# Four attention heads of a query block in a row: one finish for the four, the least score as bias, one dummy product

## What is computed

```python
def masked_softmax(s, mask):
    s = jnp.where(mask, s, NEG_INF)
    e = jnp.where(mask, jnp.exp(s - jnp.max(s, -1, keepdims=True)), 0.0)
    return e / jnp.maximum(jnp.sum(e, -1, keepdims=True), 1e-30)
...
# MLA, a block of 128 queries: q and k 96 wide
p = masked_softmax(s.astype(jnp.float32) * scale, k_pos[None, :] <= q_pos[:, None])
return jnp.einsum('bhqk,bkhd->bqhd', p.astype(v.dtype), v)
...
# NSA: compressed keys (31), selected blocks, window; a gate each
o = g[:, :, 0] * o_cmp + g[:, :, 1] * o_slc + g[:, :, 2] * o_win
...
# DSA: an index score picks the 128 best keys of each query
rel = jax.nn.relu(jnp.einsum('bqhd,bsd->bqhs', qi, k_idx).astype(jnp.float32))
score = jnp.einsum('bqh,bqhs->bqs', wi, rel)
score = jnp.where(k_pos[None, None, :] <= q_pos[None, :, None], score, NEG_INF)
_, idx = lax.top_k(score, n_top)
```

## Time and profile before

| | |
|---|---|
| time, median of 3 runs | 3823.72 us (3822.14 to 3828.15) |
| the profiled execution | 3826.97 us, span 3825.2 us |
| TensorE matmuls | 3499.9 us busy, 91% of the span |
| TensorE weight loads | 2786.0 us, 73% |
| VectorE | 1767.2 us, 46% |
| ScalarE | 1441.1 us, 38% |
| GpSimd | 181.0 us, 5% |
| mean granted clock of TensorE | 0.95 of the full one |

### The profile page before, as it was taken

How to read it: one execution, slowest core, us unless ns; L and a number is a source line. 1 busy time by engine, 2 the same in 40 slices (tenths; PEclk the granted TensorE clock), 3 DMA queues, 4 the chain that set the end, 5 groups by cost and what they waited for, 6 DMA issues and landing times. The chain is left out here.

```text
span 3825.2 us, 44194 instructions
## 1 busy us (share of the span) xinstructions
PE 3499.9 (91%) x16088; PEld 2786.0 (73%) x16126; DVE 1767.2 (46%) x2931; ACT 1441.1 (38%) x2357; POOL 181.0 (5%) x127
## 2 busy tenths in 40 slices
PE   7999889988999899989898899969999897889998
PEld 5888666766888688867576688847777675677886
DVE  4333447735333433342883533346665446444333
ACT  3332325454332333232446433235555335423321
POOL 0001011002001000100200200100000000000000
PEclk9999998989999999999898999989999998899999
DMA  3232210002232233222000222211121222222231
GB/s 132 96 103 90 94 61 1 1 19 76 99 103 95 67 99 103 95 91 74 1 1 12 72 97 99 99 43 62 62 68 62 71 74 69 76 73 94 99 103 68
DMA packets 75812, 277.38 MB, mean 73 GB/s; under 512 B 12432, under 2 KB 13968, under 8 KB 74896
## 3 DMA queue, kind: packets, MB, share of 16 engines
q1 hardware_dynamic: 75664, 275.45, 21.7%
HBM read 273.32 MB, written 2.10 MB: 72 GB/s over the span
## 5 line engine op out<-in xcount | busy, mean ns | idle before, releaser
L318 DVE TENSOR_TENSOR wlo<-raw,whi 128x1024 fp32r<-128x1024 f32 (+2 forms) x464 | 609.9, 1314 | 1019.6 <-ACT whi L314 1019.5
L346 PE MATMUL ps<-xh,whi 128*128 128x512 f32 x2384 | 941.7, 395 | 50.8 <-DVE wlo L318 38.2
L347 PE MATMUL ps<-xl,whi 128*128 128x512 f32 x2384 | 934.0, 392 | 0.0
L348 PE MATMUL ps<-xh,wlo 128*128 128x512 f32 x2384 | 933.7, 392 | 0.0
L314 ACT ACTIVATE whi<-raw 128x1024 fp32r<-128x1024 f32 (+2 forms) x464 | 515.3, 1111 | 621.5 <-PE ps L348 613.5
L346 PEld LDWEIGHTS ps<-xh,whi 128*128 128x128 f32 x2384 | 451.8, 190 | 154.1 <-DVE wlo L318 30.2
L347 PEld LDWEIGHTS ps<-xl,whi 128*128 128x128 f32 x2384 | 451.8, 190 | 95.9 <-issue 2.9
L348 PEld LDWEIGHTS ps<-xh,wlo 128*128 128x128 f32 x2384 | 451.2, 189 | 94.9
L346 PE MATMUL ps<-ffn_hh,whi 128*128 128x512 f32 x880 | 345.4, 393 | 11.1 <-DVE ffn_hl L719 11.1
L347 PE MATMUL ps<-ffn_hl,whi 128*128 128x512 f32 x880 | 343.1, 390 | 0.0
L348 PE MATMUL ps<-ffn_hh,wlo 128*128 128x512 f32 x880 | 343.1, 390 | 0.0
(11 more groups left out here) (361 smaller groups left out, 4535.5 us busy)
## 6 DMA issues: line engine op xcount, KB each, us to landing
raw<-in_ffn_up SPq DMA_DIRECT2D x216, 512.0 KB, 3.4
raw<-in_ffn_down SPq DMA_DIRECT2D x80, 704.0 KB, 4.0
raw<-in_ssm_in SPq DMA_DIRECT2D x44, 512.0 KB, 3.4
raw<-in_mix_in SPq DMA_DIRECT2D x40, 512.0 KB, 3.4
raw<-in_lru_in SPq DMA_DIRECT2D x20, 512.0 KB, 3.3
raw<-in_mix_out SPq DMA_DIRECT2D x16, 512.0 KB, 3.6
raw<-in_ssm_out SPq DMA_DIRECT2D x16, 512.0 KB, 3.3
raw<-in_lru_out SPq DMA_DIRECT2D x8, 640.0 KB, 3.9
```

What stands on the lines that cost most here:

```text
L318: dve.tensor_tensor(self.core.wlo[:, u % HALF, 0:width], self.core.raw[:, u, 0:width], self.core.whi[:, u % HALF, 0:width].bitcast(F32), A ...
L346: pe.matmul(out, c.whi[:, h, w], xh[:, k0 + k], start=first and k == 0, stop=False)
L347: pe.matmul(out, c.whi[:, h, w], xl[:, k0 + k], start=False, stop=False)
L348: mm = pe.matmul(out, c.wlo[:, h, w], xh[:, k0 + k], start=False, stop=last and k == nk - 1)
```

## The change

- The units stand in groups of four: the four heads of one query block in one branch. MLA's four blocks come first, then for each block of NSA its compressed, selected and window group, then DSA's four blocks.
- The scale is taken into the queries with a minus sign (where they are split or evacuated), and the masks are added with the opposite sign through a negative identity. So the scores are negative, the least of a row takes the place of the greatest, and it is the bias of the exponential (scale -1) as it stands: `bias` is gone. The compressed units get a 32nd column with a bound for rows without any key.
- The four heads of a group write their values into one bank, 256 columns, and their sums into one tile of four columns. `finish` runs once for a group: clamp (compressed groups), reciprocal, gate, one product of 256 columns with the factors repeated over 64 columns each, and, for selected and window groups, a separate addition. It stands between `largest` and `take` of the unit 4n + 5, with n the group.
- `keep_clock` issues one dummy product a unit instead of two.
- Two further phases (stick breaking, L1383, and the state-space groups, L1801) use the negative identity with their masks' signs turned; the set-up makes the bf16 constants with two activations instead of one.

```diff
-                act.activation(c.kb_all[:], c.consts[:, 0:N_BF16 * P], ACT.Copy).then_inc(ph["kb_done"], 1)
+                act.activation(c.kb["nident"], c.k["ident"], ACT.Copy, scale=-1.0).then_inc(ph["kb_done"], 1)
+                act.activation(c.kb_all[:, P:], c.consts[:, P:N_BF16 * P], ACT.Copy).then_inc(ph["kb_done"], 1)
...
+    def group(mixer, b, q, k, mask, at, width, v, gate=None, first=True, least=None):
+        units = [dict(q=q(h), k=k(h), mask=mask, at=at, width=width, least=least or width, v=v(h), h=h) for h in range(HEADS)]
+        groups.append(dict(units=units, mixer=mixer, b=b, gate=gate, first=first, clamp=least is not None))
+    for b in range(QB):
+        own, past = slice(b * P, (b + 1) * P), slice(0, (b + 1) * P)
+        group(0, b, lambda h: [m.qm[:, h, own]], lambda h: [m.km[:, h, past]], c.kb["negd"], b * P, (b + 1) * P,
+              lambda h: [m.vm[:, j, h * HD:(h + 1) * HD] for j in range(b + 1)])
+    for b in range(QB):
+        own, past = slice(b * P, (b + 1) * P), slice(0, (b + 1) * P)
+        q = lambda h: part(NSAQ + h // 2, h, own)
+        group(1, b, q, lambda h: part("kc", h, slice(0, NCMP + 1)), c.kb["cmpm"][:, b * (NCMP + 1):(b + 1) * (NCMP + 1)], 0, NCMP,
+              lambda h: [m.vc[:]], gate=m.tok[:, b, GATE:GATE + HEADS], least=NCMP + 1)
+        for br, (kt, vt) in enumerate(((KSLC, VSLC), (KWIN, VWIN))):
+            g = GATE + (br + 1) * HEADS
+            group(1, b, q, lambda h: part(kt, h, past), c.kb["negd"], b * P, (b + 1) * P,
+                  lambda h: [m.tok[:, j, vt:vt + HD] for j in range(b + 1)], gate=m.tok[:, b, g:g + HEADS], first=False)
+    for b in range(QB):
+        own, past = slice(b * P, (b + 1) * P), slice(0, (b + 1) * P)
+        group(2, b, lambda h: part(DSAQ + h // 2, h, own), lambda h: [x[64 * (h % 2):64 * (h % 2) + 64, past] for x in m.split[DSAK][:2]],
+              c.kb["negd"] if b == 0 else allowed[b], 0, (b + 1) * P, lambda h: [m.tok[:, j, DSAV:DSAV + HD] for j in range(b + 1)])
+    return groups
...
-                    keep_clock(c, pe, 6 + u % 2, 2)
+                    keep_clock(c, pe, 6 + u % 2, 1)
...
-                    if u >= 2:
-
-                        pe.wait_ge(ph["y_done"], u - 1)
+                    if u % HEADS == 0 and u >= 2 * HEADS:
+                        pe.wait_ge(ph["y_done"], u // HEADS - 1)
                     w = min(P, x["width"])
+                    h = x["h"]
                     for j, v in enumerate(x["v"]):
-                        mm = pe.matmul(c.ps[:, 4 + u % 2, 0:HD], pt[0:w, u % 2, j * P:(j + 1) * P], v, start=j == 0, stop=j == len(x["v"]) - 1)
+                        mm = pe.matmul(c.ps[:, 4 + u // HEADS % 2, h * HD:(h + 1) * HD], pt[0:w, u % 2, j * P:(j + 1) * P], v, start=j == 0, stop=j == len(x["v"]) - 1)
...
-                    act.wait_ge(ph["nmax_done"], u + 1)
+                    act.wait_ge(ph["least_done"], u + 1)
+                    if u % HEADS == 0 and u >= 2 * HEADS:
+                        act.wait_ge(ph["rinv_done"], u // HEADS - 1)
                     if u >= 3:
 
                         act.wait_ge(ph["t_done"], u - 2)
-                    act.activation(p[:, u % 3, 0:x["width"]], c.ps[:, u % 4, 0:x["width"]], ACT.Exp, scale=x["scale"],
-                                   bias=stat[:, u % 4, 1:2], accum_out=stat[:, u % 4, 2:3]).then_inc(ph["exp_done"], 1)
+                    act.activation(p[:, u % 3, 0:x["width"]], c.ps[:, u % 4, 0:x["width"]], ACT.Exp, scale=-1.0,
+                                   bias=least[:, u % 4:u % 4 + 1], accum_out=total[:, u // HEADS % 2, x["h"]:x["h"] + 1]).then_inc(ph["exp_done"], 1)
...
-                def maximum(u):
+                def minimum(u):
                     x = units[u]
-                    s = u % 4
                     dve.wait_ge(ph["scores_done"], u + 1)
-                    dve.reduce_max(stat[:, s, 0:1], c.ps[:, u % 4, 0:x["width"]], AXX).then_inc(ph["max_done"], 1)
-
-                def bias(u):
-                    x = units[u]
-                    s = u % 4
-                    dve.wait_ge(ph["max_done"], u + 1)
-
-                    dve.tensor_scalar(stat[:, s, 1:2], stat[:, s, 0:1], -x["scale"], 1e27, ALU.mult, ALU.min).then_inc(ph["nmax_done"], 1)
-
-                def clamp_sum(u):
-                    dve.wait_ge(ph["exp_done"], u + 1)
-                    if units[u]["clamp"]:
-                        total = stat[:, u % 4, 2:3]
-                        dve.tensor_scalar(total, total, 1e-30, None, ALU.max).then_inc(ph["sum_done"], 1)
-
-                def invert_sum(u):
-                    if units[u]["clamp"]:
-                        dve.wait_ge(ph["sum_done"], sum(y["clamp"] for y in units[:u + 1]))
-                    dve.reciprocal(stat[:, u % 4, 3:4], stat[:, u % 4, 2:3]).then_inc(ph["rinv_done"], 1)
-
-                def gate_scale(u):
-                    dve.wait_ge(ph["rinv_done"], u + 1)
-                    if units[u]["gate"] is not None:
-                        dve.tensor_tensor(stat[:, u % 4, 4:5], stat[:, u % 4, 3:4], units[u]["gate"], ALU.mult).then_inc(ph["scale_done"], 1)
-
-                def finish(u):
-
-                    x = units[u]
-                    scale = stat[:, u % 4, 3:4]
-                    if x["gate"] is not None:
-                        scale = stat[:, u % 4, 4:5]
-                        dve.wait_ge(ph["scale_done"], sum(y["gate"] is not None for y in units[:u + 1]))
-                    dve.wait_ge(ph["pv_done"], u + 1)
-                    col = x["mixer"] * HEADS * HD + x["h"] * HD
-                    out = m.y[:, x["b"], col:col + HD]
-                    if x["first"]:
-                        dve.tensor_scalar(out, c.ps[:, 4 + u % 2, 0:HD], scale, None, ALU.mult).then_inc(ph["y_done"], 1)
+                    if u >= 4:
+                        dve.wait_ge(ph["exp_done"], u - 3)
+                    dve.tensor_reduce(least[:, u % 4:u % 4 + 1], c.ps[:, u % 4, 0:x["least"]], AXX, ALU.min).then_inc(ph["least_done"], 1)
+                def finish(n):
+                    g = groups[n]
+                    tot, inv = total[:, n % 2], inverse[:, n % 2]
+                    dve.wait_ge(ph["exp_done"], HEADS * (n + 1))
+                    if g["clamp"]:
+                        dve.tensor_scalar(tot, tot, 1e-30, None, ALU.max).then_inc(ph["sum_done"], 1)
+                        dve.wait_ge(ph["sum_done"], sum(y["clamp"] for y in groups[:n + 1]))
+                    dve.reciprocal(inv, tot).then_inc(ph["rinv_done"], 1)
+                    dve.wait_ge(ph["rinv_done"], n + 1)
+                    if g["gate"] is not None:
+                        dve.tensor_tensor(inv, inv, g["gate"], ALU.mult).then_inc(ph["scale_done"], 1)
+                        dve.wait_ge(ph["scale_done"], sum(y["gate"] is not None for y in groups[:n + 1]))
+                    dve.wait_ge(ph["pv_done"], HEADS * (n + 1))
+                    heads = "p (h d) -> p h d"
+                    src = c.ps[:, 4 + n % 2, 0:HEADS * HD].rearrange(heads, d=HD)
+                    col = g["mixer"] * HEADS * HD
+                    out = m.y[:, g["b"], col:col + HEADS * HD]
+                    factor = inv.unsqueeze(2).broadcast_to([P, HEADS, HD])
+                    if g["first"]:
+                        dve.tensor_tensor(out.rearrange(heads, d=HD), src, factor, ALU.mult).then_inc(ph["y_done"], 1)
                     else:
-
-                        dve.wait_ge(ph["y_done"], u)
-                        dve.scalar_tensor_tensor(out, c.ps[:, 4 + u % 2, 0:HD], scale, out, ALU.mult, ALU.add).then_inc(ph["y_done"], 1)
+                        dve.tensor_tensor(part[:].rearrange(heads, d=HD), src, factor, ALU.mult).then_inc(ph["part_done"], 1)
+                        dve.wait_ge(ph["part_done"], sum(not y["first"] for y in groups[:n + 1]))
+                        dve.wait_ge(ph["y_done"], n)
+                        dve.tensor_tensor(out, out, part[:], ALU.add).then_inc(ph["y_done"], 1)
...
-                        maximum(u + 2)
-                    if u >= 1:
-                        clamp_sum(u - 1)
+                        minimum(u + 2)
                     largest()
-                    if u + 2 < n:
-                        bias(u + 2)
-                    if u >= 1:
-                        invert_sum(u - 1)
+                    if u % HEADS == 1 and u > HEADS:
+                        finish(u // HEADS - 1)
                     take()
-                    if u >= 1:
-                        gate_scale(u - 1)
-                    allow()
-                    if u >= 1:
-                        finish(u - 1)
                     if u < len(splits) - n_index:
                         lo(n_index + u)
-                for last in (clamp_sum, invert_sum, gate_scale, finish):
-                    last(n - 1)
+                    allow()
+                finish(len(groups) - 1)
```

(34 more changed lines are left out.)

51 lines of the change are left out of this document (19 added, 32 removed).

## The result

The changed kernel takes 3948.8 us (3945.0 to 3949.4) against 3823.3 us before: 1.032 times as long, 95% interval 1.031 to 1.034. The forecast of 3803 us was wrong by 146 us, on the side of rival B. The profiled execution took 3948.96 us with a span of 3947.3.

A forecast was written before the change was run, and what follows sets the result against it. VectorE bounds the 48 top-k rounds, TensorE the units after them. Two layers of -9.4 and -1.1 us plus 0.2 us of set-up give -20.8 us: 3823.72 becomes 3803 us, range 3793 to 3817.

The forecast's parts named there:

- rival B: TensorE's clock falls in units 16 to 47: 17 us a layer, 3837 us, chance 0.09; in part 3811 us, chance 0.08.
- the sum: All terms over both layers and set-up, -20.8 us: span 3804.4 us, median 3803 us, chance 0.50.
- stage one: Reduce of unit 2 to reduce of unit 49, VectorE-bound under top-k rounds: 92.4 us becomes 83.0 a layer.
- stage two: Reduce of unit 49 to last output, TensorE-bound: 62.8 us a layer, forecast 1.1 us less.
- Finish: Stage one, between MAX8 and the take: 11 four-head finishes on VectorE add 8.1 us a layer.
- rival C: Finish is dear, by slow broadcast product or VectorE waiting for value products: 2 to 6 us a layer, 3810, chance 0.13.
- Bias and reciprocal: Removed on VectorE in stage one; under MAX8's latency, so worth 0, bounds 0 to 0.12 us a unit.
- rival E: Removed small operations were worth their starts: 0.12 us x 47 = 5.6 us a layer, 3792 us, chance 0.07.
- Order: Blocks in order: stage one's VectorE reduces 1.6 us less, stage two's TensorE work 6.1 us more, a layer.
- Dummies of stage two: Second dummy removed on TensorE: 0.215 us x 30 units, 6.4 us less a layer.
- The order's absorption: MLA's four widest units: TensorE's excess of some 5 us taken as absorbed, bounds 0 to 6.
- rival D: VectorE idles under MLA's wide units: +6 us a layer, 3815 us, chance 0.13; sign: first sixteen units over 28 us.

The follow-up runs named there:

- Run 4: The changed kernel with two dummy products in units 12 to 47 and one in all others; 3809.1 us.
- run 6: The changed kernel with two dummies a unit, each using 32 rows of the array instead of 128; 4120.7 us.
- run 7: Run 4 with a 128x1 multiply and reciprocal on constants put back between MAX8 and the take in every unit; 3863.7 us.
- Run 11: The kernel before with units sorted by group, three dummies in units 16 to 47 and two elsewhere; 3831.4 us.
- Run 1: The changed kernel with the second dummy product put back in every unit; 3821.8 us.
- run 9: The changed kernel with the second dummy only in the twelve compressed units before unit 48; 3929.4 us.
- run 8: The changed kernel with two dummies in units 16 to 47, none from unit 56 on, one in the others; 3800.1 us.
- run 3: The kernel before with its 80 units sorted by group, two dummies a unit, nothing else changed; 3892.3 us.
- run 12: Run 7 with three dummies in units 16 to 47; 3814.5 us.
- run 2: The kernel before with one dummy product a unit instead of two; 3911.9 us.

## Why the prediction was wrong

**The step that failed.** The changed kernel's span is 142.9 us longer than the sum's 3804.4 us. Run 4, which is the same kernel with the clock held, has 3804.9. Against run 4 the changed kernel loses 16.8 and 13.3 us in stage one and 57.6 and 54.3 us in stage two, 142.0 us together. So the whole miss is the clock. Rival B named it and its place: it priced 17 us a layer for units 16 to 47, and stage one lost about this, though the level fell only at unit 21 and 23, so the price per unit was too low. What it left out was stage two, four fifths of the damage. The step was this sentence: "a TensorE at half level is nearly full, which should bring the level back". In the changed kernel TensorE was full, or nearly so, at the half level until the first layer's last output, 186.5 us after the fall, and for 174 us in the second layer before the level came back. It argued from the return at the beginning of the phase; there, though, TensorE had other work (the index scores, MLA's fp32 products), and run 6 shows that even there the return hangs on the dummies: with 32 rows in each it didn't come. From this followed the wrong price (3837 instead of 3949). The chance of 0.09 for a whole fall was low for the same reason: it rested on the same sentence and on stage one's dummies lying under VectorE's work, by which "dropping one is worth nothing there as such". It was hidden in time, and it was what held the clock.

The Trainium skill (TensorE: Matmul & The Clock Gate, HAM oscillation) ties the fall to idle gaps of TensorE, and the same page's table of the two states (under What's actually happening) calls the half level that of an idle engine. Here the clock fell in a stretch in which the profile shows no hole, and stayed at half with TensorE busy for 67.00 of 67 us. The measurement decides. The page's passage on a cycling PSUM queue, which I cited for B, tells of a clock that swings between the levels; in the changed kernel it fell once in each phase and stayed for 201 and 174 us.

**The rest of the sum held.** With the clock held (run 4) stage one lasts 83.6 and 84.4 us, forecast 83.0; stage two changed by -1.2 us, forecast -1.1; the span of the profiled execution is 3804.9, forecast 3804.4. That the spans agree to 0.5 us is in part luck: stage one was 0.6 and 1.4 us over its forecast, and the profiled execution of run 4 is the fastest of its five, while that of before, 3827.0 us, lies 3.3 us above its median. By medians it is less good: 3809.1 against 3825.0 on that chip, so 15.9 us gained of the 20.8 forecast. By terms:

- *Finish, rival C.* VectorE's time line of run 4 has an MLA finish, then a plain round, a compressed finish and one of a selected group:

```profile
639.68 0.42 DVE L1237 MAX8 idx_top<-idx_score 128x8 f32<-128x256 f32 x1
640.13 0.09 DVE L1244 MATCH_VALUE_LOAD idx_score<-idx_top,idx_score 128x8 f32 x1
...
641.14 0.42 DVE L1237 MAX8 idx_top<-idx_score 128x8 f32<-128x256 f32 x1
...
641.66 0.42 DVE L1282 TENSOR_TENSOR mix_y<-ps,att_inverse 128x256 f32<-128x256 f32 x1
642.01 0.08 DVE L1244 MATCH_VALUE_LOAD idx_score<-idx_top,idx_score 128x8 f32 x1
...
652.39 0.55 DVE L1237 MAX8 idx_top<-idx_score 128x8 f32<-128x384 f32 x1
652.98 0.09 DVE L1244 MATCH_VALUE_LOAD idx_score<-idx_top,idx_score 128x8 f32 x1
...
655.40 0.55 DVE L1237 MAX8 idx_top<-idx_score 128x8 f32<-128x384 f32 x1
...
656.46 0.42 DVE L1282 TENSOR_TENSOR mix_y<-ps,att_inverse 128x256 f32<-128x256 f32 x1
656.80 0.08 DVE L1244 MATCH_VALUE_LOAD idx_score<-idx_top,idx_score 128x8 f32 x1
...
661.49 0.55 DVE L1237 MAX8 idx_top<-idx_score 128x8 f32<-128x384 f32 x1
...
662.35 0.42 DVE L1284 TENSOR_TENSOR att_part<-ps,att_inverse 128x256 f32<-128x256 f32 x1
662.81 0.43 DVE L1287 TENSOR_TENSOR mix_y<-mix_y,att_part 128x256 f32<-128x256 f32 x1
663.15 0.08 DVE L1244 MATCH_VALUE_LOAD idx_score<-idx_top,idx_score 128x8 f32 x1
```

The whole finishes come to 4 x 0.42, 3 x 0.81 and 4 x 1.07, 8.4 us; 8.1 was forecast. The product of 256 columns with the broadcast factor takes 0.42 us; 0.41 was estimated, and the 0.97 to 1.63 us of the earlier trace rows doesn't apply. From MAX8 to the match load a round of 256 columns takes 0.87 us with an MLA finish and 0.45 without, so 0.42 more (forecast 0.40); the compressed one 1.40 instead of 0.59, 0.81 more (0.78); the selected one 1.66, so 1.07 more (1.05).
- *Bias and reciprocal, rival E.* Worth 0 in a plain round and 0.12 us in one with a finish (run 7). The prediction took 0 for all; rival E's 0.12 was the right size for 10 rounds of 47.
- *Order.* Run 11: stage two +5.6 us (forecast +6.1), stage one -1.4 and -0.6 (forecast -1.6).
- *Dummies of stage two.* Run 1 to run 4: 68.3 to 61.9 us for 31 units, 0.21 us each; 0.215 was forecast.
- *The order's absorption, rival D.* The reduces of units 2 to 18 take 27.4 and 28.2 us in run 4, about the 28 named as its sign. But VectorE does stand still behind MLA's widest units, in the compressed ones:

```profile
643.99 0.19 DVE L1260 TENSOR_REDUCE att_least<-ps 128x1 f32<-128x32 f32 x1 [0.53 <-PE ps L1138]
...
646.27 0.19 DVE L1260 TENSOR_REDUCE att_least<-ps 128x1 f32<-128x32 f32 x1 [0.90 <-PE ps L1138]
...
648.54 0.19 DVE L1260 TENSOR_REDUCE att_least<-ps 128x1 f32<-128x32 f32 x1 [0.96 <-PE ps L1138]
...
650.00 0.42 DVE L1282 TENSOR_TENSOR mix_y<-ps,att_inverse 128x256 f32<-128x256 f32 x1 [0.72 <-PE ps L1161]
```

The first three are D's. The fourth is rival C's other half: a finish waits for its last value products, and the match load is queued behind it. These four make 3.1 of the 5.4 us for which VectorE is idle in stage one; no other of its idle times there is above 0.15 us. In the second layer it is idle for 6.2 us. Before it was 4.8 and 4.3. So the mechanisms of D and C were there, but their waits largely took the place of the 3.9 us that the sum had kept for other idle times. VectorE is idle for 0.6 and 1.8 us more than before, not for six.

**What stays open.** Why the fall comes at unit 21 in one run and at unit 35 or 42 in another, and how much work of which height of the array a stretch needs, these runs don't settle. They bracket it for this order and this pace: in units 16 to 47 one dummy is too few (the changed kernel, run 9), two hold in runs 1, 4 and 8, but not with the slower VectorE of the kernel before (run 3), and with two small operations more only in one layer of two (run 7). Three held in the two runs that gave them to all 32 units (11 and 12).

## What to carry to other kernels

A product without a result may be hidden in time and still hold the clock: before one is dropped, ask what is left on the array in the narrowest stretch at the slowest pace, and price the whole way to where the level can return, not the stretch of the fall. Busy time doesn't tell whether the level will hold or return. Put dummies where another engine sets the pace (here under the top-k rounds, where the second costs little: stage one of run 4 takes 83.6 and 84.4 us with it, 83.0 by the sum without it) and leave them out where TensorE's own wide products hold the level: that, with the change, makes 3793 us out of 3823.

## What the runs showed of the hardware

- The granted clock fell without a long idle time of TensorE: at 653.4 us in the changed kernel, at 683.0 in run 2, at 691.2 in run 3. Before the first the profile shows no hole at all, 8.40 of 8.40 us busy and a matmul started at least every 0.22 us; before the other two the longest idle time in the 13 us ahead of the fall was 0.41 and 0.25 us.
- The same instructions hold either level: stage two with one dummy ran for 61.8 us at 1.00 and for 119.5 us at 0.50. Twenty-one dummies in a row (6.69 us) moved it from the one to the other.
- Dummies on 32 rows don't do what dummies on 128 rows do, with the same columns: run 6 was at 0.50 for both phases, 78.00 of 78 us busy.
- Two small operations on VectorE between MAX8 and the match load cost nothing where nothing else stands there (0.59 us from the one to the other with and without them), and 0.12 us where a finish already fills MAX8's latency (0.99 against 0.87 us).
